# One loop of count plus one for the expert rounds on TensorE and ScalarE, with a round's six ring slots given back together

## The reference, cut to what matters

```python
g, u = jnp.split(xb @ w_up[e], 2, axis=-1)
return (jax.nn.silu(g) * u) @ w_down[e]
```

```python
a = jnp.einsum('nd,edf->nef', t, w_gate[g])
b = jnp.einsum('nd,edf->nef', t, w_up[g])
hid = jax.nn.silu(a) * b * combine[:, g, :, None]
y = y + jnp.einsum('nef,efd->nd', hid, w_down[g])
```

## Time and profile before

| what | value |
|---|---|
| median of 3 runs | 1766.58 us |
| profiled execution, its span | 1765.07 us, 1763.3 us |
| TensorE matmul busy, weight load busy | 1387.5 us, 736.8 us |
| VectorE, ScalarE, GpSimd busy | 450.8, 396.6, 41.7 us |
| moved by DMA | 477.40 MB, mean 271 GB/s |
| mean granted TensorE clock | 0.915 |
| expert stage, first layer | 390 to 892 us, 379 GB/s |
| expert stages, second block | 1062 to 1314 us, 380 GB/s; 1482 to 1764 us, 316 GB/s |

### The profile page before, as it was taken

One profiled execution on the slowest core, in us unless ns is written; L12 is line 12 of the kernel. 1 busy time (PEld: TensorE's weight loads), 2 busy tenths in 40 slices (PEclk: granted clock), 3 DMA queues, 4 the chain that ended last, 5 costly groups with the idle time before them and its releaser, 6 DMA issues.

```text
span 1763.3 us, 31667 instructions
## 1 busy us (share of the span) xinstructions
PE 1387.5 (79%) x12322; PEld 736.8 (42%) x12323; DVE 450.8 (26%) x1373; ACT 396.6 (22%) x766; POOL 41.7 (2%) x80
## 2 busy tenths in 40 slices
PE   3899987867666676698968879878789887998775
PEld 2555454444332242355546444333337534433332
DVE  0103346542111121122234522111122523111112
ACT  1101214112111121122223312212232412222221
POOL 2000201000000000000000000000000000000000
PEclk9999968979999999999979879989898896999997
DMA  9957210119999999969793125999992220779994
GB/s 319 327 215 286 71 49 1 63 49 379 410 409 410 409 410 410 410 258 409 308 349 143 53 96 239 418 417 418 418 341 102 96 78 34 286 312 418 417 417 173
DMA packets 125615, 477.40 MB, mean 271 GB/s; under 512 B 8977, under 2 KB 19470, under 8 KB 108990
## 3 DMA queue, kind: packets, MB, share of 16 engines
q1 hardware_dynamic: 122496, 468.61, 67.5%
q0 software_dynamic: 2160, 6.51, 1.4%
q10 hardware_dynamic: 910, 1.59, 0.3%
HBM read 474.71 MB, written 1.97 MB: 270 GB/s over the span
## 4 chain that ended last, share of the span: by engine, by line
PE 52%; DMA 21%; SPq 11%; DVE 6%; issue 5%; ACT 2%; PEld 2%; ACTq 0%; PEldq 0%; POOL 0%; DVEq 0%
DMA ring<-in_w_up 14%; SPq L461 10%; PE psum L1678 5%; PE psum L673 5%; PE psum L995 5%; PE psum L1007 4%; PE psum L982 3%; PE psum L955 3%; DMA ring<-in_w_expert_up 3%; PE psum L1025 3%; PE psum L1674 3%; DMA ring<-in_w_expert_down 2%; PE psum L1235 2%; PE psum L1018 2%; PE psum L1247 2%
## 5 line engine op out<-in xcount | busy, mean ns | idle before, releaser
L995 PE MATMUL psum<-ring,arena 128*32 128x256 f32 x2624 | 171.9, 401 | 75.5 <-DMA ring<-in_w_expert_up 75.3
L1007 PE MATMUL psum<-ring,arena 128*32 128x256 f32 x2432 | 163.2, 428 | 50.5 <-DMA ring<-in_w_up 50.3
L1156 DVE TENSOR_TENSOR arena<-arena,psum 128x128 f32<-128x128 f32 x79 | 22.8, 288 | 609.9 <-ACT arena L1087 609.9
L995 PEld LDWEIGHTS psum<-ring,arena 128*32 128x32 f32 x2624 | 78.3, 113 | 153.6 <-DMA ring<-in_w_expert_up 99.6
L1007 PEld LDWEIGHTS psum<-ring,arena 128*32 128x32 f32 x2432 | 95.6, 122 | 107.9 <-issue 77.3
L982 PE MATMUL psum<-arena 32*128 32x256 f32 (+1 forms) x992 | 127.6, 469 | 2.1 <-ACT arena L1094 2.1
L955 PE MATMUL psum<-xn,arena 128*32 128x256 f32 (+1 forms) x992 | 127.6, 482 | 0.0
L1087 ACT ACTIVATE arena<-psum 128x128 f32<-128x128 f32 x79 | 21.9, 277 | 421.2 <-PE psum L995 230.7
L1087 ACT ACT_TABLE_LOAD x79 | 101.4, 1283 | 7.5 <-issue 6.2
L1678 PE MATMUL psum<-ring,hT 128*128 128x512 f32 x224 | 97.7, 593 | 0.0
L973 PE MATMUL psum<-const_sb,arena 128*128 128x128 f32 x158 | 33.2, 293 | 74.7 <-issue 48.4
(11 more groups left out here) (327 smaller groups left out, 1531.8 us busy)
## 6 DMA issues: line engine op xcount, KB each, us to landing
ring<-in_w_expert_up SPq DMA_DIRECT2D x128, 1024.0 KB, 18.2
ring<-in_w_expert_down SPq DMA_DIRECT2D x64, 1024.0 KB, 18.2
ring<-in_w_gate SPq DMA_DIRECT2D x64, 1024.0 KB, 16.1
ring<-in_w_up SPq DMA_DIRECT2D x64, 1024.0 KB, 18.1
ring<-in_w_down SPq DMA_DIRECT2D x64, 1024.0 KB, 20.7
ring<-in_w_mod SPq DMA_DIRECT2D x12, 2048.0 KB, 14.6
ring<-in_w_in SPq DMA_DIRECT2D x6, 2048.0 KB, 9.1
ring<-in_w_out SPq DMA_DIRECT2D x6, 2048.0 KB, 13.0
```

Of the source, the lines that this page charges most:

```text
L995: mm = pe.matmul(out_(j), chosen_rows(k, 0), wt[:, kk, :, j, :], start=(k == 0), stop=(k == KD - 1))
L1007: mm = pe.matmul(out_(j), chosen_rows(k, e), wt, start=(k == 0), stop=(k == KD - 1))
```

## The change

TensorE and ScalarE keep one copy of a round, in a loop of `n + 1`. What the last copy did beside computing moves into `done(own)`, behind the loop: `next_extra`, and on TensorE the wait for the round's last matmul and one increase of `piece_used` by 6. VectorE keeps both copies, since its last round reads another expert's ranks. The order and number of matmuls, activations and loads stay.

```diff
-        def each_round(eng, name, at, which, per_turn, round_):
+        def each_round(eng, name, at, which, per_turn, round_, last_round=None, done=None):
...
                     n = eng.snap(more)
-                    with eng.If(n > 0):
-                        with eng.Fori(0, n):
+                    if last_round is None:
+                        with eng.Fori(0, n + 1):
                             round_(turn, i, own, False)
-                    round_(turn, i, own, True)
+                    else:
+                        with eng.If(n > 0):
+                            with eng.Fori(0, n):
+                                round_(turn, i, own, False)
+                        last_round(turn, i, own, True)
+                    if done:
+                        done(own)
...
-                        if last and piece < 3:
-                            mm.then_inc(sems["piece_used"], 1)
...
-                    if last and piece == 0:
-                        mm.then_inc(sems["piece_used"], 1)
...
                 combine()
-                if last:
-                    next_extra(pe, "pe", own + 1)
                 pe.wait_ge(sems["w_hid"], v)
                 pe.transpose(U[:, 0:P], hid, ident).then_inc(sems["w_ht"], 1)
-                if last:
-
-                    pe.sem_inc(sems["piece_used"], 1 if which == 1 else 4)
...
-                down(turn, i, last)
-                if last:
-
-                    pe.wait_ge(sems["w_y"], v)
-                    pe.sem_inc(sems["piece_used"], which)
+                down(turn, i)
+
+            def done(own):
+
+                next_extra(pe, "pe", own + 1)
+                pe.wait_ge(sems["w_y"], pe.snap(win))
+                pe.sem_inc(sems["piece_used"], ROUND)
...
-            each_round(pe, "pe", at, which, 2, round_)
+            each_round(pe, "pe", at, which, 2, round_, done=done)
...
-                if last:
-                    next_extra(act, "act", own + 1)
...
-            each_round(act, "act", at, which, 1, round_)
+            each_round(act, "act", at, which, 1, round_, done=lambda own: next_extra(act, "act", own + 1))
...
-            each_round(dve, "dve", at, which, 1, round_)
+            each_round(dve, "dve", at, which, 1, round_, last_round=round_)
```

More of the change, by code:

```diff
@@ L984, in combine, with up @@
                 return mm
-            def up(turn, i, last):
+            def up(turn, i):
                 out_ = lambda j: U[quadrant(j), 0:2 * P].rearrange("p (u n) -> p u n", u=2)
@@ L1008, in up, with down @@
                 mm.then_inc(sems["w_up"], 1)
-            def down(turn, i, last):
+            def down(turn, i):
                 if which == 2:
@@ L1039, in round_ @@
                 pe.wait_ge(sems["w_got"], v + part)
-                up(turn, i, last)
+                up(turn, i)
                 pe.wait_ge(sems["w_sel"], v + (part + 1))
```

## The result

The changed kernel takes 1787.07 us (median of 4 runs, 1784.87 to 1789.90) against 1767.01 us before: ratio 1.0117, 95% interval 1.0083 to 1.0150. The forecast was 1786.5 us. The profiled execution took 1786.35 us, its span is 1784.5 us; before it was 1765.07 us.

The account below looks back on a forecast made before the run. Weight loads (DMA) were taken to bound one-round experts, TensorE the extra rounds. First layer 9.7, second stage 5.1 and third 5.2 us sum to 20.0 us (16.4 to 23.1): 1786.5 us against the median, mechanism range 1781 to 1791, overall 1777 to 1796.

Parts of the forecast that it names:

- The main step: Expert stages: a slot's later return moves time where the load queue is empty, nothing where it holds a few loads; 76%.
- The two rivals in which the ring absorbs the move: Late give-back hidden by the twelve-slot ring: fully, 1755 us, 5%; or mostly, 0 to 8 us, about 1772 us, 11%.
- the one with exposed engine work: Behind last rounds: `next_extra` not hidden, 0.8 us at 12 places, up to 10 us, 1790 to 1797 us; 6%.
- Start of the first layer: Rounds 0 and 1: stalls go, first loads issued 2.3 to 3.6 us later; net 1.3 us later, carried to round 25.
- The steady stretch: First layer behind its start: give-back 1.5 us behind an expert's last piece, 15.4 us of loads still queued; no cost.
- End of the first layer: Rounds 26 to 40: slots return late to an empty queue, rounds 34 and 40 wait for pieces; +8.4 us.
- just fits: Round 31, first layer: runs from 800.8 to 809.3 us, needs its last piece at 808.3, which lands at 808.2; no wait.
- Second and third stage: First loads behind round 0 (second) and restart behind round 7 (third) wait for the round's end: 5.1 and 5.2 us longer.
- the rival with code loads at the new loop's edge: Back edges of the new loops: body fetched again, 3.3 to 6.1 us each, 33 to 60 us, 1800 to 1827 us; 2%.
- The rule of a two-page window: Taken branches outside two pages stall for a fetch: 29 later skips at 6.07 us, 176 us; not used in the sum.
- The saving per expert: Between two experts: a taken branch of 0.21 us replaced by cheaper steps; about 0.1 us saved, bounds 0 and 0.2.

Follow-up runs that it names:

- the second trace: The changed kernel measured again beside four further kernels on another chip, against the kernel before: 1784.21 us, ratio 1.0118.

## Why the prediction was right

**What decides.** The main step held: a slot's return costs time where the queue of loads is empty, and nothing where it holds a few. The two-copy kernel with the late give-back alone loses 30.3 us, and returning four slots earlier in the one-copy kernel takes the loss away, to within the 3.6 us of its interval. Between them little room is left for a cost of the loop, the branches or `next_extra`. The two rivals in which the ring absorbs the move, and the one with exposed engine work, are refuted by these runs. What the sum left out is the clock: it took the durations of the one trace of before, and at several places told below the changed kernel ran the same matmuls at the other of the clock's two levels.

**Start of the first layer.** 1.3 us were forecast in bounds 0.4 to 2.6; measured 2.4 in both traces. The size of the parts was right: the stalls went (1.06 and 0.66 us of idle instead of 4.34 and 6.70), round 0 took 8.5 us at the full clock, and the first issue came 4.2 us later in a trace that was itself 1.45 us late. The loads were right too. Round 25, before and changed:

```profile
750.22 1.07 PE L995 MATMUL psum<-ring,arena 128*32 128x256 f32 x16 [1.49 <-DMA ring<-in_w_expert_up]
```

```profile
752.94 1.94 PE L1001 MATMUL psum<-ring,arena 128*32 128x256 f32 x16 [0.62 <-DMA ring<-in_w_expert_up]
...
758.29 1.93 PE L1029 MATMUL psum<-ring,arena 128*32 128x256 f32 x32
```

The fourth piece comes 2.7 us later, less the 1.45 us: the forecast 1.3, and 1.3 in the second trace as well. The steady stretch behind the start, in which every slot returned late, added nothing. The other 1.1 us arises in round 25 itself: `up` and the gather run at the lower clock in the changed kernel (0.50 from 751 to 756 us) and at the full one before (1.00 from 750 to 753), and `down`, which before waited for the last piece, no longer does. TensorE, not the load, ends the round.

**End of the first layer.** 8.4 us were forecast in bounds 6.8 to 9.5; measured 11.9 and 9.5. The landing times held, and so did the places. Round 34 was forecast 3.1 us longer and took 4.3 and 3.3 us more; round 40 was forecast 5.9 us longer and took 7.4 and 6.5 us more. Two things were missing from the term. Round 31, where the last piece "just fits", waited 0.41 us in the first trace and not in the second. And the waits can have a price behind them: in round 34 of the first trace the last 16 matmuls of `up` and the gather take 1.88 and 1.95 us instead of 1.07 and 1.05, 1.7 us together. In the second trace they take 1.07 and 1.04 us behind the same waits, and most of the slow matmuls are in round 40. The stage windows before had shown that price: a mean clock of 0.90 to 0.95 where TensorE waits for weights, 1.00 where it does not the earlier trace rows.

**Second and third stage.** 5.1 and 5.2 us were forecast; measured 4.0 and 2.1, and 5.0 and 4.9. The event that SyncE waits for is as worked out. Between the last row of PE in a round and the issue lie 0.3 us:

```profile
1092.12 1.92 PE L1022 MATMUL psum<-ring,arena 128*32 128x512 f32 x16
```

ends at 1094.04, and SyncE issues at 1094.35. But the 5.2 us of the second stage were forecast with a round 0 as long as in the trace of before, where its `up` ran partly at the lower clock (mean granted clock 0.72 from 1068 to 1074 us; in the changed trace 1.00 from 1083 to 1095). This is that `up` before and then in the changed kernel:

```profile
1068.93 5.35 PE L1007 MATMUL psum<-ring,arena 128*32 128x256 f32 x64
```

```profile
1084.06 3.66 PE L1011 MATMUL psum<-ring,arena 128*32 128x256 f32 x64
```

So the first issue comes 6.9 us behind the stage's start before and 10.8 us in both changed traces, 3.9 us later. The kernel with only `next_extra` moved gives back as before and had this `up` in 3.88 us; it issued 5.3 us behind the start, and against it the delay is 5.5 us. The last wait of the stage, in round 14, ends 4.7 and 4.3 us later behind the stage's start (4.7 to 5.4 forecast). From there to the end it is 43.8 us before, 43.1 and 41.7 changed; round 14's `up` alone takes 5.69, 5.10 and 3.66 us. The stage's 4.0 and 2.1 us are thus the restart less what the clock gave. In the third stage the restart comes 5.7 and 5.6 us later behind the stage's start (5.2 forecast).

**Branches and code.** The one-copy loop's branch in the changed kernel, over all 79 rounds:

```profile
L923 PEldq COMPARE_BRANCH  x79: 67/76/231, 399.1 to 1762.9; - x79
...
L918 PEldq COMPARE_BRANCH  x32: 73/216/231, 410.1 to 1765.0; - x32
```

The second row is the loop over turns. Before, the first skip took

```profile
L922 PEldq COMPARE_BRANCH  x1: 3313/3313/3313, 390.1 to 390.1; - x1
```

and the second 6.07 us. No pass of either loop is near that, so the rival with code loads at the new loop's edges is refuted. The rule of a two-page window that the prediction takes from the Trainium skill (Runtime: NRT & Kernel Launch, Instruction fetch mechanics) is not borne out by the trace either. The row that bears on it most is L918, which jumps back over all the code of a turn (567 instructions where no round is extra) in 0.23 us at most.

The saving per expert was 0.14 to 0.18 us (0.83 to 0.69; in the second block 0.85 to 0.67, and 1.21 to 1.04 at a turn's end). At a turn's end in the first layer the gaps ahead of rounds 31, 34 and 39 were 1.42, 1.28 and 1.19 us and are now 1.20 each. 0.1 was taken throughout.

**What was luck.** The sum of 20.0 us met the measured 20.1, the difference of the medians, by errors that cancel. In the profiled execution (+21.3 us) they are 1.1 and 3.5 us too little in the first layer, 1.1 too much in the second stage, 3.5 us that the straight stretches gave back, and 1.45 us lost ahead of the first expert stage, where the code is the same. The second chip's trace has +16.4 us in all, its runs +18.5. How little a single trace fixes a stage is seen in the kernel with only `next_extra` moved: its time is that of before, and its second stage is 2.0 us shorter.

## What to carry to other kernels

A ring that holds two units of work hides a late give-back only while its queue of loads is not empty. Look for the restarts, that is for the stretches in which the DMA engines rest, and charge there the full delay of the first slot returned. Give slots back as soon as the last reader is known to be through, even if that needs a branch in the loop's last pass: here one branch and one wait in a single-copy loop turned 1.2% lost into 0.3 to 0.4% won, while the copies of the code themselves mattered mostly on their first pass. And where a term is the distance between two events of one trace, look at the clock between them: here the same round took 12.2 or 10.5 us, and a third of a restart's price hung on it.

## What the runs showed of the hardware that was not expected

The same straight code takes a different time from run to run with the time that TensorE spends at its lower clock. The stretch between the second and the third expert stage took 168.7, 170.6, 173.4 and 174.5 us in four traces (the first and the last are of one and the same kernel), and in them the granted clock was at its lower level for 44.4, 47.8, 58.0 and 61.4 us: 17 us more at half clock go with 6 us more time. The stretch between the first and second stage ran from 175.4 to 180.3 us with 51.2 to 64.9 us at the lower level. So 3 us can be won or lost in such a stretch without touching it, more than half a restart term of this case. What decides when the clock falls there (the time at which the stretch starts, or chance) no run here separates.
